# Two chained model blocks on one core: block 2's attentions reordered over eight units, block 1's first attention rows issued inside the last merge projection

## What is computed

```python
def hybrid_layer(x, ...):                      # l = 0, 1
    q, k, v, gate_a, u_b, gate_b, q_idx, k_idx, w_idx, merge = split(rms_norm(x) @ w_in)
    attn = indexer_sparse_attention(...)       # 8 heads of 64, one shared k and v, 256 keys of a row kept
    y_a = (attn * silu(gate_a)) @ w_a
    y_b = (pooled * silu(gate_b)) @ w_b
    g_a, g_b = split(sigmoid(merge))
    return x + (g_a * y_a + g_b * y_b) @ w_out
```

```python
h = layer_norm(x)
qa, ka, va, qb, kb, vb, ga, gb = split(h @ w_in + b_in)
y_na  = neighbourhood_attention(qa, ka, va, rpb) @ w_branch_na
y_swa = windowed_gqa_with_sink(rot(qb), rot(kb), vb, sink) @ w_branch_swa
h = layer_norm(ALPHA * h + (sigmoid(ga) * y_na + sigmoid(gb) * y_swa) @ w_out + b_out)
h = layer_norm(ALPHA * h + square(relu(h @ w_ff1 + b_ff1)) @ w_ff2 + b_ff2)
```

## Time and profile before

| | |
|---|---|
| median of the runs | 3622.06 us (3620.77 to 3625.8) |
| the profiled execution | 3625.04 us, span 3623.2 us |
| PE busy | 3385.8 us, 93% of the span |
| PE weight loads | 2939.8 us, beside the matmuls |
| DVE, ACT, POOL busy | 1859.3, 1265.2, 1215.9 us |
| mean granted TensorE clock | 0.966 of full speed |
| DMA | 230.64 MB moved, mean 64 GB/s |

### The profile page before, as it was taken

The page is one execution under the profiler, slowest core; times in us unless marked ns, Lnnn a source line. Parts: engine busy times, 40 slices in busy tenths (PEclk is TensorE's granted clock), DMA queues, the critical chain, the costliest instruction groups (busy, mean ns, idle before and its releaser), DMA issues.

```text
span 3623.2 us, 45938 instructions
## 1 busy us (share of the span) xinstructions
PE 3385.8 (93%) x18148; PEld 2939.8 (81%) x18148; DVE 1859.3 (51%) x3271; ACT 1265.2 (35%) x1946; POOL 1215.9 (34%) x835
## 2 busy tenths in 40 slices
PE   5899999999989999999899999998899899999997
PEld 4788999989878899999866787776777588888885
DVE  4578999653456899975342354444533512000014
ACT  4553221452364322135223344344422521222223
POOL 3324533215332363311533323211253432323231
PEclk8999999999999999999999999999899899999998
DMA  5101222205210112210423212011143111111111
GB/s 138 33 24 41 62 74 93 73 1 177 95 48 24 36 54 80 92 60 1 153 71 138 64 34 50 30 47 44 68 134 99 29 47 47 47 47 47 47 52 48
DMA packets 284181, 230.64 MB, mean 64 GB/s; under 512 B 31473, under 2 KB 257408, under 8 KB 283584
## 3 DMA queue, kind: packets, MB, share of 16 engines
q1 hardware_dynamic: 253792, 116.40, 11.9%
q0 software_dynamic: 23264, 85.89, 6.8%
q10 hardware_dynamic: 6912, 25.41, 1.7%
HBM read 177.29 MB, written 52.36 MB: 63 GB/s over the span
## 4 chain that ended last, share of the span: by engine, by line
PE 72%; POOL 7%; issue 7%; DVE 7%; ACT 4%; DMA 1%; SPq 1%; ACTq 0%; POOLq 0%; DVEq 0%
PE big L529 54%; PE small L666 3%; PE small L576 3%; PE big L629 2%; POOL wsp L1517 2%; PE big L645 2%; PE big L552 2%; PE small L738 2%; PE big L562 1%; DVE X L2213 1%; POOL tm L1637 1%; POOL H L1517 1%; PE small L811 1%; SPq L475 1%; DMA tm<-gate_b_scratch 1%
## 5 line engine op out<-in xcount | busy, mean ns | idle before, releaser
L529 PE MATMUL big<-H,wsp 128*128 128x348 f32 (+2 forms) x9984 | 1956.0, 356 | 60.0 <-POOL H L1517 31.0
L529 PEld LDWEIGHTS big<-H,wsp 128*128 128x128 f32 (+1 forms) x9984 | 1719.7, 190 | 270.9 <-issue 34.6
L1517 POOL TENSOR_TENSOR wsp<-raw,wsp 128x1024 fp32r<-128x1024 f32 (+2 forms) x246 | 548.8, 2231 | 1524.4 <-ACT wsp L1004 1514.4
L529 PE MATMUL big<-SP,wsp 128*128 128x512 f32 x1920 | 451.0, 395 | 0.0
L529 PEld LDWEIGHTS big<-SP,wsp 128*128 128x128 f32 x1920 | 359.1, 187 | 90.4 <-issue 1.7
L1004 ACT ACTIVATE wsp<-raw 128x1024 fp32r<-128x1024 f32 (+2 forms) x246 | 238.1, 968 | 517.5 <-PE big L529 377.5
L2142 DVE MAX8 top<-SC 128x8 f32<-128x272 f32 (+6 forms) x448 | 368.2, 822 | 0.0
L2148 DVE MATCH_REPLACE8 SC<-top,SC 128x272 f32<-128x272 f32 (+6 forms) x448 | 364.8, 814 | 0.0
L2307 DVE TENSOR_TENSOR X<-X,big 128x1024 f32<-128x1024 f32 (+1 forms) x26 | 29.6, 1139 | 476.1 <-PE big L529 475.9
L666 PE MATMUL small<-V,PT_a 128*128 128x64 f32 x1152 | 146.1, 272 | 0.1
L666 PEld LDWEIGHTS small<-V,PT_a 128*128 128x128 f32 x1152 | 141.3, 192 | 3.7 <-ACT PT_a L1097 0.4
(11 more groups left out here) (249 smaller groups left out, 3852.7 us busy)
## 6 DMA issues: line engine op xcount, KB each, us to landing
raw<-in_w_in SPq DMA_DIRECT2D x108, 512.0 KB, 3.9
raw<-in_w_ff SPq DMA_DIRECT2D x64, 512.0 KB, 4.1
raw<-in_w_out SPq DMA_DIRECT2D x24, 512.0 KB, 5.3
gate_b_scratch<-tm POOLq DMA_DIRECT2D x16, 522.0 KB, 3.1
gate_a_scratch<-tm ACTq DMA_DIRECT2D x16, 522.0 KB, 2.7
tm<-gate_a_scratch POOLq DMA_DIRECT2D x16, 522.0 KB, 3.8
tm<-gate_b_scratch POOLq DMA_DIRECT2D x16, 522.0 KB, 4.6
tm<-xT_scratch POOLq DMA_DIRECT2D x16, 522.0 KB, 5.3
```

The lines of the kernel that those rows point to most:

```text
L529: mm = pe.matmul(dst(o, width), w[wp][:, k, 0:cols], rhs(xp, k)[:, t0:t0 + width], start=(k == 0 and i == 0), stop=(k == rows - 1 and i == 2))
L1517: pool.tensor_tensor(dst, src, hi.bitcast(F32), ALU.subtract).then_inc(*S.inc(name, *key))
```

## The change

- **Block 2, scores and rows.** Units take turns between two banks of `big[0]`; keys beyond 512 go to a bank of `big[1]`. Rows have four buffers (`rows_b`), the exponent is written in place.
- **Block 2, ends.** Values of eight units collect side by side in one bank of `small2`; the normalising, the sink's terms and the turning back are done once for eight units. The turning back of a chunk's last eight stands after three chunks of the next projection.
- **Block 2, beginnings.** `nav` goes to `small2`; its last two chunks stand after the first two units' scores, and its transposes after the third's. For the window kind one chunk of the m2 job stands ahead of the rotation, five behind it, and two after the first two units' scores. `swk`'s rotation stands behind `swv`, and the transposes of v behind the first `swq`. The m2 job beside the units has its chunks at steps 1, 2, 4, 5, 7, 8, 10, 11.
- **Block 1.** Chunks 0 and 1 of `ma` 7, then scores of unit 0, chunks 2 to 4, scores of unit 1, chunks 5 to 7, scores of unit 2. ACT copies `ma` 7 without its sigmoid at step 2 of the attention, and applies the sigmoid after it was read back, ahead of `ya` 7's product. `weight_hi` and `weight_lo` behind `ma` 7 and the four loads of silu(gate_a) move to step 4 of the attention.

```diff
 # PE, block 2
+                def scores(k):
+                    u = units[k]
+                    if k >= 2:
+                        pe.wait_ge(*S.at("masked", *units[k - 2]["key"]))
+                    near = min(u["n"], BANK)
+                    for part in range(2):
+                        mm = pe.matmul(big[0][:, k % 2 * BANK:k % 2 * BANK + near], u["q"], u["k"][part][:, 0:near],
+                                       start=(part == 0), stop=(part == 1))
...
+                for k in range(N + 3):
+                    if k == 2:
+                        for e in free[1] or []:
+                            pe.wait_ge(*S.at(*e))
+                    if 2 <= k < N + 2:
+                        transposes(k - 2)
+                    if k < N:
+                        scores(k)
+                    if k <= 3:
+                        before(k)
+                    if 3 <= k < N + 3:
+                        values(k - 3)
+                    if k >= 6 and closes_b(units[k - 6]):
+                        turn_back(units[k - 6])
...
+            def project_at(job, emptied_by, at, last=None):
+                claim(job, emptied_by, at)
+                part_of(job, range(3))
+                if last is not None:
+                    turn_back(last)
+                part_of(job, range(3, KC))
...
+                project_at(("nak", c), [("raw_copied", "nak", c)], 1, last)
+                project_at(("naq", c), [("raw_copied", "naq", c)], 0)
+                claim(("nav", c), [("v_biased", "nav", c)], 2)
+                part_of(("nav", c), range(6))
                 for e in (("q_stacked", "naq", c), ("k_split", "nak", c)):
                     pe.wait_ge(*S.at(*e))
...
+                project_at(("swq", c), [("raw_copied", "swq", c)], 0 if c else 1, last if c else None)
+                if c == 0:
+                    turn_values("swv", 0, 0)
+                first = ("m2", M2_BEFORE[c])
+                claim(first, [("m2_sigmoid", M2_BEFORE[c])], 1)
+                part_of(first, range(1))
+                rotate2(("swq", c), 0)
+                part_of(first, range(1, 6))
                 for e in (("q_stacked", "swq", c), ("k_split", "swk", 0)):
                     pe.wait_ge(*S.at(*e))
 # PE, block 1
+                for k, chunks in enumerate((range(2), range(2, 5), range(5, KC))):
+                    mm = products(("ma", l, 7), hi_lo(H), pieces1, None, chunks)
+                    if k == 0:
+                        pe.wait_ge(*S.at("ma_sigmoid", l, 6))
+                        pe.wait_ge(*S.at("q_stacked", "q", l, 3))
+                        pe.wait_ge(*S.at("k_split", "k", l))
+                        pe.wait_ge(*S.at("mask0_in", l))
+                    if k < 2:
+                        scores(k)
+                mm.then_inc(*S.inc("projected", ("ma", l, 7)))
+                scores(2)
+                pe.wait_ge(*S.at("gate_kept", "ma", l))
 # ACT, block 1
+                    if m == 7:
+                        act.wait_ge(*S.at("mix_in1", "b", l, 7))
+                        act.activation(tm[:, 1, :], tm[:, 1, :], ACT.Sigmoid).then_inc(*S.inc("late_sigmoid", "ma", l))
 # DVE, block 2, once for eight units
+                    step(dve.reciprocal(head_inv[:, at, :], total))
+                    dve.tensor_tensor(by_unit(Ob_b[:, at, :]), by_unit(small[at]),
+                                      head_inv[:, at, :].unsqueeze(2).broadcast_to([P, HEADS, HD]), ALU.mult)\
+                        .then_inc(*S.inc("normed_out", *block))
 # POOL, the store that stands ahead of the next chunk's bias loads
                 store(f"attn_out{c % 2}", (c,), at_d[c], tm[:, c % 2, 0:SEQ],
-                      [("gated", phases[("n",)][16 * c + 14]["i"])])
+                      [("gated", "n", c, 1)])
```

More of the change, by code:

```diff
@@ L543, in plain, with turn_back @@
                 mm.then_inc(*S.inc(name, *key))
-            def attention(units, values_ready, beside=None):
-                def scores(u):
-                    if u["i"] >= 1 and u is not units[0]:
-                        pe.wait_ge(*S.at("masked", u["i"] - 1))
-                    mm = None
-                    for part in range(2):
-                        for o, w, k in u["k"][part]:
-                            mm = pe.matmul(big[0][:, o:o + w], u["q"], k, start=(part == 0), stop=(part == 1))
-                    mm.then_inc(*S.inc("logits", u["i"]))
-                def transposes(u, prev):
-                    pe.wait_ge(*S.at("exped", u["i"]))
-                    if prev is not None:
-                        for e in moved_events(prev):
+            def turn_back(u):
+                pe.wait_ge(*S.at("normed_out", *block_b(u)))
+                for i in range(4):
+                    mm = pe.transpose(small[slot_b(u)][:, i * P:(i + 1) * P], Ob_b[:, slot_b(u), i * P:(i + 1) * P], ident[:])
+                mm.then_inc(*S.inc("out_turned", *block_b(u)))
@@ L936, in by_chunk @@
-            def by_chunk(kind, before):
-                units = phases[(kind,)]
-                for c in range(4):
-                    part = [u for u in units if u["c"] == c]
-                    before(c)
-                    if kind == "n":
-                        attention(part, ("v_ready", "nav", c))
-                    else:
-                        attention(part, ("v_ready", "swv", 0), M2_BESIDE[c] if c < 3 else None)
-            by_chunk("n", before_na)
-            project(("swk", 0), hi_lo(H), pieces2, [("raw_copied", "swk", 0)])
@@ new lines, in _ @@
+                last = attention([u for u in units_b["n"] if u["c"] == c], before_na)
+            project_at(("swk", 0), [("raw_copied", "swk", 0)], 1, last)
+            project_at(("swv", 0), [("v_biased", "swv", 0)], 0)
+            rotate2(("swk", 0), 2)
+            for c in range(4):
+                project_at(("swq", c), [("raw_copied", "swq", c)], 0 if c else 1, last if c else None)
[6 more added lines that the diff above has]
+                part_of(first, range(1, 6))
@@ L956, in before_swa @@
                 for e in (("q_stacked", "swq", c), ("k_split", "swk", 0)):
                     pe.wait_ge(*S.at(*e))
-            by_chunk("s", before_swa)
+                def before_swa(k):
+                    if k in (0, 1):
+                        part_of(first, [6 + k])
+                    elif k == 3 and c == 0:
+                        pe.wait_ge(*S.at("v_ready", "swv", 0))
+                last = attention([u for u in units_b["s"] if u["c"] == c], before_swa, M2_BESIDE[c] if c < 3 else None)
@@ L1678, in _ @@
                 for k in range(len(units) + 8):
+                    if k == 4:
+                        after(("ma", l, 7))
+                        for c in range(4):
+                            load(f"silu_in{c % 2}", (l, c), tm[:, c, :], sg_d[c],
+                                 [(f"gate_out{c % 2}", "a", l, c),
+                                  (f"ma_out{c % 2}", l, 6 + c) if c < 2 else (f"yb_out{c % 2}", l, 4 + c)])
                     if k < len(units):
```

402 lines of the change are left out of this document (216 added, 186 removed).

## The result

The changed kernel takes 3603.93 us (median of 4 runs, 3597.27 to 3604.58), the kernel before beside it 3623.93 (3620.77 to 3626.55): a ratio of 0.9942, with a 95% interval of 0.9927 to 0.9957. So it is faster by 20 us, 0.6%; 7 had been forecast. Its profiled execution was the quickest of the four, 3597.27 us with a span of 3595.4, 27.8 under the span of before.

A forecast was written before the change was run, and what follows sets the result against it. PE was taken as the bound, busy 93%, so only its waits and lower clock could be won. 24 + 18.8 - 10.8 - 7.8 - 1 - 2.9 - 21.3 + 8 = 7.0 us gained: 3615, range 3606 to 3627.

The forecast's parts named there:

- nav for POOL in chunks 1 to 3: Neighbourhood chunks 1 to 3: PE newly waits 3.6 us for nav's weights behind POOL's queue, 10.8 lost in all.
- window scores for q: Ahead of window chunks: first scores newly wait 3.4 us for q, formerly covered by three more m2 chunks.
- block 1's unit 1 for unit 0's mask: Block 1's attention start: unit 1's scores wait for unit 0's masked rows, a new PE wait of 4.8 us.
- the out job for the late sigmoid: Block 1, end of ya 7: table load and sigmoid come before DVE's product, 1.75 us lost per layer.
- The waits between units: Inside block 2's attentions: three groups of PE waits, together 28.7 us; 24 us gained net from removing them.
- block 1's first values: Block 1's attention: first values at 667.9 against 668.20, 0.3 us gained per layer.
- The rival by which a second bank only brings PE to the moves sooner: Inside block 2's attentions: inner waits stay, only 5 of the 24 us gained, 3634 us, slower; chance 0.17.
- window chunk 3 without an m2 job: Inner-waits rival's test (chance 0.17): window units without an m2 chunk beside them still take more than 1.8 us each.
- the clock's balance: Whole kernel: 21.3 us lost to lower clock behind new waits, 8 gained at swq behind four chunk ends.
- a mean clock above 0.966: Whole kernel: a rise of the mean clock above 0.966 would show the forecast wrong.
- The 7.8 for the clock at nav: Neighbourhood chunks 1 to 3: lower clock behind the new nav wait, charged at 2.6 us in each of three.
- The rival's mechanism: Neighbourhood chunks 1 to 3: POOL and DVE exclude each other, nav wait 5.9 us, 2.3 more each, 3622; chance 0.08.

The follow-up runs named there:

- the bank by itself: Block 2's part alone, with unit k's scores waiting again for the masked rows of unit k - 1, as if one bank: 3595.19 us, ratio 0.9922.
- block 2's part alone: The changed kernel with its block 1 part undone, block 1's attention beginning behind all of `ma` 7 as before: 3593.12 us, ratio 0.9916.
- the early sigmoid: The changed kernel with ACT applying the sigmoid of `ma` 7 at once inside the attention: 3600.48 us, ratio 0.9937.
- nav's weights first: Block 2's part alone with nav's low part ahead of the bias tables in POOL's queue: 3578.85 us; with the m2 job also whole before window scores: 3563.91.

## Why the prediction was right and wrong

**Right in its mechanisms.** Every wait that it said would come came in its place, and all but one within a third of its size: nav for POOL in chunks 1 to 3, 3.6 forecast and 3.4 found, from 11.3 and 11.2 us of POOL's work; window scores for q, 3.4 forecast, 2.9 found in chunks 1 and 2 and 1.3 in chunk 3; block 1's unit 1 for unit 0's mask, 4.8 and 3.3; the out job for the late sigmoid, 1.75 and 2.2 (2.43 - 0.23). The waits between units went, but block 1's first values, forecast 0.3 earlier, came 1.8 later. The rival by which a second bank only brings PE to the moves sooner had its price wrong, since most of the inner gain came, but the bank by itself was worth no more than 2: right about the bank, wrong to think that the gain hung on it. In the chunk by which it wanted to be judged, window chunk 3 without an m2 job, its sign came in part. The chunk takes 28.4 us for 16 units where it took 35.1, 1.8 a unit on the mean. PE in order of time in the changed kernel, the values of two units that lie eight apart:

```profile
2586.98 0.78 PE L611 MATMUL small<-V,PT_b 128*128 128x64 f32 x6
...
2603.24 0.78 PE L611 MATMUL small<-V,PT_b 128*128 128x64 f32 x6
```

In the middle of the chunk a unit takes 2.0 us, and PE waits 0.8 to 1.4 ahead of every second one's transposes. Who sets that pace is not shown; the profile names nobody.

**The step that failed: the clock's balance.** The sum set 21.3 us lost behind new waits against 8 gained behind chunk ends. It charged each new wait for a stretch at the lower level, 1.2 GHz, and looked for old stretches of that kind, which would go, at one place only. New drops cost what was charged where they came, 1.7 to 2.0 ahead of each window chunk against 2. But the trace of before had more old ones:

Ahead of y1, the kernel before, and after (the stretch, us, busy PE, PEld, DVE, ACT, POOL, clock):

```profile
2633.50:2638.50 5.00, 5.00 (x13) 3.94 (x14) 0.29 (x1) 1.06 (x1) 2.86 (x2) 0.52 0.51 203
```

```profile
2614.90:2619.00 4.10, 4.10 (x20) 3.24 (x18) 1.82 (x2) 1.59 (x2) 1.99 (x1) 1.00 0.00 0
```

A clock of 0.52 over 5.0 us loses 2.4, most of the 3.4 behind the last values. Before neighbourhood chunks 1 and 3 the old kernel took 44.6 and 44.8 and before chunk 2 it took 43.0: 1.7 each, gone as well. And block 1's start already paid: the clock of 0.50 in the earlier trace rows is 3.3 us lost, and the sum put 2.75 on top of it for a longer wait. In the changed kernel that stretch is shorter, not longer:

```profile
657.10:664.30 7.20, 7.14 (x34) 6.82 (x35) 1.47 (x4) 2.52 (x4) 0.39 (x2) 0.76 0.00 0
```

That loses 1.7. The largest old loss lay inside window chunk 3: a clock of 0.74 over 35.1 us, 9.0 lost, where the changed kernel has 0.92 over 28.4 and loses 2.3. The sum had no term for it. Before and after in the two profiled executions, us (lost to the clock is a stretch's length times what its granted clock lacks to 1):

| stretch | length | PE idle | lost to the clock |
|---|---|---|---|
| ahead of the first neighbourhood values | 2061.7, 2067.9 | 144.4, 150.3 | 64.9, 66.6 |
| inside the neighbourhood attentions | 132.7, 130.6 | 0.5, 0.0 | 0.3, 0.0 |
| between the neighbourhood chunks | 132.4, 127.6 | 12.2, 13.4 | 6.6, 0.0 |
| inside the window attentions | 136.2, 111.6 | 16.4, 8.3 | 10.8, 2.3 |
| ahead of the window chunks | 169.5, 170.5 | 23.0, 25.3 | 12.0, 7.1 |
| behind the last values | 990.6, 987.2 | 40.9, 40.9 | 27.7, 22.6 |
| sum | 3623.2, 3595.4 | 237.4, 238.2 | 122.1, 98.5 |

The forecast named a mean clock above 0.966 as a sign that it was wrong, and that sign came: 0.973. The clock gave 23.6 us where the sum had it take 13.3; idle time gave nothing where the sum had 20.3 net. So the sum erred in both halves and in opposite directions, and that 7 and 20 lie as near as they do is in part luck. One reason for the second error can be read in the trace of before: the wait terms are differences of lengths, and these held low clock. The 13.0 us ahead of the first values of neighbourhood chunk 1 contain a drop that costs 3.1. Some 5 us of the 28.6 by which PE's busy time fell belong neither to the clock nor to idle time; what they are is not shown.

**The 7.8 for the clock at nav was the most that it costs, and not its mean.** In the profiled execution it did not occur at all. In the trace of block 2's part alone the three chunks lie 2.6, 1.4 and 1.6 us above 42.5, in that with the early sigmoid 2.5, 0.5 and 2.6: 5.6 in each. The changed kernel's other three runs took 3603.53 to 3604.58 us at mean clocks of 0.968 to 0.970, the profiled one 3597.27 at 0.973. I take most of the difference, 6.3 to 7.3 us, to be these three drops. That is argued and not shown: only one of the four runs has a trace, and the clock drops elsewhere too, so that up to block 2 equal code differs by 2.5 us from trace to trace.

**The rule on shared access holds; its price was misjudged.** SBUF — State Buffer (the Trainium skill, *Who interferes with whom*) has a DVE instruction with two SBUF inputs contend with a GpSimd one that reads SBUF, for ports that only one of them holds at a time. The prediction made of it that POOL's four operations and DVE's four on k follow one another, with a wait of 5.9 at nav; the wait was 3.38. Three of DVE's four operations in the changed kernel, which lie beside the rows of POOL above:

```profile
2117.70 1.22 DVE L2368 TENSOR_TENSOR K<-tm,K 64x1024 fp32r<-64x1024 f32 x1
2118.95 3.04 DVE L2368 TENSOR_TENSOR K<-tm,K 64x1024 fp32r<-64x1024 f32 x1
2122.03 2.35 DVE L2368 TENSOR_TENSOR K<-tm,K 64x1024 fp32r<-64x1024 f32 x1
```

POOL's two table operations in the kernel before, which began with no DVE operation on k under way:

```profile
2108.58 2.12 POOL L1741 TENSOR_TENSOR bias_e<-bias_e,colmask 128x896 f32<-128x896 f32 x1
2110.78 1.43 POOL L1743 TENSOR_TENSOR bias_i<-bias_e,rowmask 128x576 f32<-128x576 f32 x1
```

Beside DVE they take 2.95 and 2.30, 0.83 and 0.87 longer, and the weight operation takes 3.33, 0.98 longer than its 2.35 alone. When they began, at 2117.96, 2120.99 and 2123.25, the DVE operation under way had 0.96, 1.00 and 1.13 us to go: each is longer by that, less 0.13 to 0.15. Chunks 2 and 3 show the same: L1832 takes 2.70 with 0.71 to go, and 3.10 with 1.11. DVE's third and fourth are longer than 1.22 by 1.82 and 1.13, with 1.96 and 1.26 to go of POOL's. So the trace agrees with the page: the two take turns, an instruction at a time. But an engine waits only for the rest of the one instruction that the other has under way. That cost POOL 2.7 us in three pieces and not four whole operations, and the 11.3 of the sum, which counts such a piece from the earlier trace rows, was right within 0.1. POOL's first operation, a tensor_scalar, is different here: DVE's first two took 1.22 each beside it. The rival's mechanism was at work, at a lower price.

**The table load.** ACT in order of time, layer 0, ahead of the last product:

```profile
873.64 1.28 ACT L1411 ACT_TABLE_LOAD   x1
874.93 1.08 ACT L1411 ACTIVATE tm<-tm 128x1044 f32<-128x1044 f32 x1
```

The load follows the end of ACT's split of the sum by 0.02 us and the sigmoid follows the load at once: 2.37 for both, and 2.2 of it reaches PE. By ScalarE: Activation LUTs (the Trainium skill, *What ACT_TABLE_LOAD costs*) it would have been 3.1 per layer; the trace agrees with the page's load time, and shows no drain beside it here.

**Terms that were missing.** The PSUM turn of `ma` 0: 1.1 us per layer (565.31), which the new kernel shows (`claim` by number) and the sum left out. The new steps of the m2 job: 2 to 7 us. And the q wait's companion: the forecast left ACT's first exponent at 4.65 behind the m2 job, which was right (4.7 in window chunk 1, from the sigmoid's start at 2446.61 to the transposes at 2451.30) and became the largest wait that is left.

## What to carry to other kernels

When a wait is hidden behind later work, follow what the waiting instruction released: a store behind it can stand at the head of another engine's queue, and the time comes back there unless the urgent entry is put first. Cut a job so that enough of it stands ahead of a wait whose length the trace of before already shows (13.1 us from swq to q here), rather than spread it evenly. And when charging the clock for a new wait, take off what the same stretch already lost at its lower level before.

## What the runs showed of the hardware that was not expected

A wait of 3.38 us of PE, at the same instruction with the same work around it (two kernels that differ in block 1 alone), was followed by 36 matmuls of 512 columns in 8.57 us at a granted clock of 1.00 in one execution and in 11.14 us at 0.75 in another. Waits of 1.1 to 1.3 us had two outcomes as well, 1.6 us apart, within a single execution (41.7, 40.1, 41.7 between the neighbourhood chunks). With the waits gone, all six such stretches in the two profiled kernels with nav's weights first agreed within 0.01 us (38.89 to 38.90). Here, then, fewer gaps also meant less variation from chunk to chunk.

Where DVE and POOL met with instructions of two SBUF inputs, each instruction was longer by what the other's had still to go, less 0.13 to 0.15 us, five times in a row (2117.96 to 2126.58).
